# Moving the first two compressed transpositions of the next head group ahead of a turn's last gated sum and its split

## The chip, the cores and the metric

The kernel runs on one core of a Trainium2 chip. The metric is the device time of one execution in microseconds (us). Before the change the median of three runs is 2229.71 us (2229.05 to 2230.18).

## What is computed

The reference is two transformer layers (an mLSTM branch and a sliding-window attention branch, then a squared-ReLU MLP), followed by one block of sparse attention with three branches over 512 tokens and a width of 1024. Only the last block is touched here. It has 16 heads of 64 in 4 key groups of 4 heads each:

```python
q, kv, g, z = split_cols(h @ w_in, [...])
gates = jax.nn.sigmoid(g).reshape(B, S, 3, H, 1)
zs = jax.nn.silu(z).reshape(B, S, 3, H, dh)
kc = compress_kv(k_c, k_pos, k_w1, k_w2)          # 31 compressed keys
vc = compress_kv(v_c, v_pos, v_w1, v_w2)
o_cmp, p_cmp = nsa_compressed(q, kc, vc, table)   # softmax over 31 keys
sel = select_blocks(p_cmp, S)                     # S = 512 has 8 blocks, and all are taken
o_slc = nsa_selected(q, k_s, v_s, sel, table)     # so: full causal attention, keys k_s
o_win = nsa_window(q, k_w, v_w, table)            # window 512: full causal attention, keys k_w
o = jnp.stack([o_cmp, o_slc, o_win], axis=2)
y = jnp.sum(gates * o * zs, axis=2).reshape(B, S, NSA_WIDTH)
return y @ w_out
```

Everything is float32. A product is made of three passes on TensorE: both operands are split into a high part and a low rest (`hi`, `lo`), and hi x hi, lo x hi and hi x lo are summed in PSUM.

## The kernel before

**Five engines, one list of steps.** TensorE (PE), VectorE (DVE), ScalarE (ACT), GpSimd (POOL) and the queue of loads (SP) each run their own program in strict order, and semaphores join them. For the last block all of them walk one written list of steps, `NTURNS`, and each engine issues only its own share of a step. So the order of the list is the order on every engine. The list is put together by `turns()` from three tables: `NSA_FIRST` opens group 0, `NSA` is the body of groups 0 to 2 and ends with steps marked `"next"`, which belong to the group after, and `NSA_LAST` is the body of group 3. The passage from one group to the next, where steps of both alternate, is called a seam below; there are three. `('fill',)` is a slot into which `place_fill` puts the next quarter of a weight unit in a fixed sequence: `u0`, `h0`, `m1`, `u1` of `z` 0 to 5 and then of the next group's `q` 0 and 1.

**A weight unit** is a 1024 x 128 piece of the weights. A quarter of it is six 128x512 matmuls (L639 to L641). With `h0` and `u1`, ACT rounds half of the unit two further on (L1056, `w_hi`) and POOL then takes the rest (L555, `w_lo`). At `u1` of a `z` unit ACT also takes the tanh (L1103) and DVE multiplies (L1670, `sz`), which frees the PSUM bank.

**The steps by name.** `CS` the logits on the compressed keys (PE L935, 16 matmuls), then the minimum and the exponential; `cscale` sums, reciprocals and scaling of these (DVE L2144, L2145, L2150, L2151); `CT` transposes one tile of 128 tokens of them (PE L946, four matmuls), ACT copies the tile twice (L1502, L1504) and DVE subtracts for the low part (L2156); `CV` multiplies it with the values (PE L957); `cmul` adds the result into `y` (DVE L2170). `XS` is a full causal score tile (PE L967), DVE adds the bias and finds the row minimum (L2183), ACT takes the exponential (L1512); `xrec`, `xsa`, `xsp` scale it; `XT` transposes (PE L976, ACT L1525, DVE L2199), `XV` multiplies with the values (L989, L990), `xsum` adds the halves. `fmul` is the gated sum of the last branch: for the second half of the tokens DVE multiplies (L2218) and adds (L2219). `yhi` and `ylo` split `y` for the last product: for the second half ACT rounds (L1541) after L2219, and DVE takes the rest (L2222) after L1541. Nothing before the last product reads these two parts.

Score tiles use two PSUM banks in turn, and transpositions two others; a step has to wait until the consumer of the tile two before it is done. `CV` of tiles 0 and 1 waits for L2156 of its own tile. `CV` of tiles 2 and 3 waits in addition for `cmul` of tiles 0 and 1, since they share the output banks. DVE's share of `fmul` 1, `ylo` 1, `CT` and `XS` is this:

```python
elif s[0] == "CT":
    dve.wait_ge(pt_hi, pt0 + pv_index("c", qt) + 1)
    V.tensor_tensor(PTn[qt % 2][CP:CP + NC, 0, :], ps[0:NC, 4 + us[0].b, :], PTn[qt % 2][0:NC, 0, :].bitcast(F32),
                    ALU.subtract).then_inc(t_free[us[0].b], 1)
elif s == ("fmul", 1):
    link(V.tensor_tensor(ocur[:, :, cols], ocur[:, :, cols], sz[:, 4:6, cols], ALU.mult))
    V.tensor_tensor(y32[:, :, cols], y32[:, :, cols], ocur[:, :, cols], ALU.add).then_inc(y_v, 1)
elif s == ("ylo", 1):
    dve.wait_ge(y_hi_done, DEPTH * KT + it * 2 + 2)
    V.tensor_tensor(y_part(1, it, 1), y32[:, :, TOKENS[1]], y_part(0, it, 1).bitcast(F32),
                    ALU.subtract).then_inc(y_done, 1)
```

Of the kernel before, what the change touches and what calls it, by code (L numbers as in the profile page):

```python
# [72 lines left out]
def unit(kind, n):  # L73

    return [("u0", kind, n), ("h0", kind, n), ("m1", kind, n), ("u1", kind, n)]
# [51 lines left out]
        + [("TK", 2), ("TK", 3)] + unit("q", 0)[:2] + [("ngatesT",)] + unit("q", 0)[2:] + [("compress",)] + unit("q", 1))  # L127
BRANCH_PV = {"c": 0, "s": 4, "f": 14}
ITER_PV = 24
NSA_FIRST = [('ks',), ('gst',), ('kclo',), ('fill',), ('fill',), ('fill',), ('CS', 0), ('CS', 1), ('cscale', 0), ('vclo',), ('fill',), ('cscale', 1), ('fill',), ('fill',), ('gstv',)]  # L130
# [2210 lines left out]
```

## Time and profile before

| | |
|---|---|
| median of three runs | 2229.71 us |
| profiled execution | 2229.75 us, of which the span is 2228.0 us |
| PE busy | 2178.1 us (98% of the span) |
| DVE, ACT, POOL busy | 1046.1, 1085.3, 971.9 us |
| mean granted TensorE clock | 0.996 |
| CS of groups 0 to 3 starts at | 1849.52, 1928.20, 2011.44, 2094.34 us |

The profile is one execution. A row of a timeline gives the start in us from the span's start, the duration, engine, line, operation and tiles; in brackets stands the idle time of the engine just before, and the instruction that ended it. PE is busy nearly all the time, so what counts is the little idle time of PE and who ends it.

### The profile page before, as it was taken

Reading aid. Unit: us, or ns where it says so; the run is one execution under the profiler, and the core shown is the slowest. Engines: PE = TensorE matmul, PEld = TensorE weight load, DVE = VectorE, ACT = ScalarE, POOL = GpSimd, SP = SyncE. Lnnn points to the kernel's source line nnn. Section 1 sums busy time; section 2 is a strip of 40 time slices with the busy share of each in tenths; the row PEclk is TensorE's granted clock in tenths of the full one; section 3 lists DMA queues with packets and bytes.
Section 4 is the critical chain, followed back from the end, with each engine's and each line's share of the span. In section 5 each row is a group of like instructions: output and inputs, shape, how many; then the busy total and the mean of one; then the engine's idle time right before and its main releaser. Section 6 shows DMA issues by size and latency. Waiting matters only on the chain.

```text
span 2228.0 us, 31566 instructions
## 1 busy us (share of the span) xinstructions
PE 2178.1 (98%) x10287; PEld 1793.3 (80%) x10287; DVE 1046.1 (47%) x2195; ACT 1085.3 (49%) x2273; POOL 971.9 (44%) x757
## 2 busy tenths in 40 slices
PE   7999999999999999999999999999999999999997
PEld 5888888788888888888888788888888787777766
DVE  7365364523231234563563623321324726767773
ACT  5466466434232234464564624322324427787783
POOL 3333333444444444434333344544544334555544
PEclk9999999999999999999999999999999999999999
DMA  3222222223322322222322223323322431211213
GB/s 131 85 86 67 94 78 69 82 94 107 101 95 94 104 94 95 85 76 76 95 70 83 67 94 110 99 95 97 102 94 94 155 123 58 74 64 53 76 32 121
DMA packets 60288, 198.70 MB, mean 89 GB/s; under 512 B 6815, under 2 KB 13520, under 8 KB 59537
## 3 DMA queue, kind: packets, MB, share of 16 engines
q1 hardware_dynamic: 53808, 183.77, 25.2%
q10 hardware_dynamic: 6368, 13.50, 1.7%
q8 instruction: 64, 1.05, 0.2%
q14 instruction: 48, 0.39, 0.1%
HBM read 192.99 MB, written 4.26 MB: 89 GB/s over the span
## 4 chain that ended last, share of the span: by engine, by line
issue 57%; POOL 26%; PE 9%; DVE 5%; ACT 1%; POOLq 1%; DMA 0%; DVEq 0%; SPq 0%; ACTq 0%
POOL w_lo L541 26%; PE ps L639 2%; PE ps L641 2%; PE ps L640 2%; DVE Pn L2183 1%; PE ps L976 1%; PE ps L967 1%; PE ps L989 1%; DVE PTn L2199 1%; POOLq L537 1%; PE ps L990 1%; POOLq L539 1%; DMA w_raw<-w_all 0%; DVE y L2170 0%; DVE ocur L2212 0%
## 5 line engine op out<-in xcount | busy, mean ns | idle before, releaser
L541 POOL TENSOR_TENSOR w_lo<-w_raw,w_hi 128x512 fp32r<-128x512 f32 x592 | 778.4, 1322 | 1065.9 <-ACT w_hi L1056 1064.2
L639 PE MATMUL ps<-hT_hi,w_hi 128*128 128x512 f32 x1600 | 643.4, 402 | 1.9 <-DVE hT_lo L1732 1.3
L641 PE MATMUL ps<-hT_hi,w_lo 128*128 128x512 f32 x1600 | 626.0, 391 | 0.0
L640 PE MATMUL ps<-hT_lo,w_hi 128*128 128x512 f32 x1600 | 624.9, 391 | 0.0
L1056 ACT ACTIVATE w_hi<-w_raw 128x512 fp32r<-128x512 f32 x664 | 410.8, 626 | 414.1 <-PE ps L641 380.2
L641 PEld LDWEIGHTS ps<-hT_hi,w_lo 128*128 128x128 f32 x1600 | 301.0, 188 | 65.3
L639 PEld LDWEIGHTS ps<-hT_hi,w_hi 128*128 128x128 f32 x1600 | 301.5, 188 | 62.1 <-issue 2.4
L640 PEld LDWEIGHTS ps<-hT_lo,w_hi 128*128 128x128 f32 x1600 | 301.9, 189 | 57.6 <-issue 0.5
L639 PE MATMUL ps<-u_hi,w_hi 128*128 128x512 f32 x512 | 199.2, 389 | 0.0
L640 PE MATMUL ps<-u_lo,w_hi 128*128 128x512 f32 x512 | 199.2, 389 | 0.0
L641 PE MATMUL ps<-u_hi,w_lo 128*128 128x512 f32 x512 | 199.2, 389 | 0.0
L1704 DVE TENSOR_TENSOR x<-x,ps 128x512 f32<-128x512 f32 x64 | 44.0, 688 | 256.6 <-PE ps L641 256.6
L555 POOL TENSOR_TENSOR w_lo<-w_raw,w_hi 128x512 fp32r<-128x512 f32 x72 | 93.1, 1296 | 115.1 <-ACT w_hi L1056 115.1
L1677 DVE SCALAR_TENSOR_TENSOR e_buf<-ps,rs 128x512 f32<-128x512 f32 x64 | 44.3, 692 | 208.6 <-PE ps L641 208.6
L1107 ACT ACTIVATE u_hi<-e_buf 128x512 fp32r<-128x512 f32 x64 | 40.5, 633 | 173.1 <-DVE e_buf L1677 173.1
L639 PEld LDWEIGHTS ps<-u_hi,w_hi 128*128 128x128 f32 x512 | 96.1, 188 | 20.0
L640 PEld LDWEIGHTS ps<-u_lo,w_hi 128*128 128x128 f32 x512 | 96.1, 188 | 19.9
L641 PEld LDWEIGHTS ps<-u_hi,w_lo 128*128 128x128 f32 x512 | 96.1, 188 | 19.9
L1640 DVE SCALAR_TENSOR_TENSOR aq<-ps,aq 64x512 fp32r<-64x512 f32 x32 | 22.0, 689 | 149.3 <-ACT aq L1081 148.7
L1512 ACT ACTIVATE Pn<-Pn,st 128x128 f32<-128x128 f32 (+3 forms) x128 | 71.5, 559 | 25.0 <-DVE st L2183 25.0
L2183 DVE CUSTOM_DVE_ANT_0 Pn<-ps,biasn 128x128 f32<-128x128 f32 (+3 forms) x128 | 60.2, 489 | 25.2 <-DVEq L1587 24.9
L639 PE MATMUL ps<-y_hi,w_hi 128*128 128x512 f32 x176 | 68.7, 390 | 1.7 <-DVE y_lo L2222 1.7
(330 smaller groups left out, 3437.9 us busy)
## 6 DMA issues: line engine op xcount, KB each, us to landing
w_raw<-w_all SPq DMA_DIRECT2D x332, 512.0 KB, 3.3
bias<-scr_w ACTq DMA_DIRECT2D x8, 512.0 KB, 3.7
biasn<-scr_n SPq DMA_DIRECT2D x4, 1024.0 KB, 5.2
w1k<-w_in ACTq DMA_DIRECT2D x2, 1024.0 KB, 7.4
w1v<-w_in ACTq DMA_DIRECT2D x1, 2048.0 KB, 12.8
scr_x<-x ACTq DMA_DIRECT2D x1, 2048.0 KB, 7.5
x<-scr_x SPq DMA_DIRECT2D x1, 2048.0 KB, 9.2
out<-x SPq DMA_DIRECT2D x16, 128.0 KB, 1.8
```

The lines of the kernel that those rows point to most:

```text
L537: with pool.Fori(0, count) as i:
L541: nc.gpsimd.tensor_tensor(w_lo[:, h, :], raw[:, h // 2, (h % 2) * HALF:(h % 2 + 1) * HALF], w_hi[:, h, :].bitcast(F32), ALU.subtract).then ...
L555: nc.gpsimd.tensor_tensor(w_lo[:, 2 * u.b + h, :], raw[:, u.b, h * HALF:(h + 1) * HALF], w_hi[:, 2 * u.b + h, :].bitcast(F32), ALU.subtrac ...
L639: nc.tensor.matmul(ps[:, p, :], wh, hi[:, kk, :], start=(kk == 0), stop=False)
L640: nc.tensor.matmul(ps[:, p, :], wh, lo[:, kk, :], start=False, stop=False)
L641: last = nc.tensor.matmul(ps[:, p, :], wl, hi[:, kk, :], start=False, stop=(kk == KT - 1))
L1056: nc.scalar.activation(w_hi[:, 2 * p + h, :], raw[:, p, h * HALF:(h + 1) * HALF], ACT.Copy)\
L1107: nc.scalar.activation(u_hl[0][:, n, :], e_buf[:, e.b, :], ACT.Square).then_inc(u_hi_done, 1)
L1512: nc.scalar.activation(p_, p_, ACT.Exp, scale=-1.0, bias=st[:, 0, j:j + 1], accum_out=st[:, 1, j:j + 1]).then_inc(probs, 1)
L1677: V.scalar_tensor_tensor(e_buf[:, e.b, :], g, 0.0, rs[:, :], ALU.max, ALU.mult).then_inc(g_free[u.b], 1)
L1704: V.tensor_tensor(x[:, n, :], x[:, n, :], g, ALU.add).then_inc(g_free[u.b], 1)
L2183: last = V.tensor_tensor_reduce(out=Pn[:, qt % 2, hd, 0:n], in0=ps[:, 2 + b_, e * n:(e + 1) * n], in1=reverse(biasn, hd, n), scale=1.0, sc ...
```

## The change

The two `CT` steps that opened `NSA` and `NSA_LAST`, and the two fill slots beside them, are put at the end of `NSA_FIRST` and among the `"next"` steps at the end of `NSA`. In the three seams `fmul` 1 comes after them, and `yhi` 1 and `ylo` 1 after one fill slot more. In group 0 they keep their place as such, but the quarters `m1` and `u1` of `z` 1 now stand around them. The diff, cut to the places that differ (each table is one line in the source, cut by "..."):

```diff
-NSA_FIRST = [..., ('cscale', 1), ('fill',), ('fill',), ('gstv',)]
-NSA = [('fill',), ('CT', 0), ('CT', 1), ('fill',), ('XS', 's', 0, 0), ('fill',), ('XS', 's', 0, 2), ...
-       ('xsum', 'f', 3), ("next",) + ('vclo',), ('fmul', 1), ("next",) + ('fill',), ("next",) + ('cscale', 1),
-       ("next",) + ('fill',), ("next",) + ('fill',), ("next",) + ('gstv',), ('yhi', 1), ('ylo', 1)]
-NSA_LAST = [('CT', 0), ('fill',), ('CT', 1), ('fill',), ('XS', 's', 0, 0), ('XS', 's', 0, 2), ...
+NSA_FIRST = [..., ('cscale', 1), ('fill',), ('fill',), ('gstv',), ('fill',), ('CT', 0), ('CT', 1), ('fill',)]
+NSA = [('XS', 's', 0, 0), ('fill',), ('XS', 's', 0, 2), ...
+       ('xsum', 'f', 3), ("next",) + ('vclo',), ("next",) + ('fill',), ("next",) + ('cscale', 1),
+       ("next",) + ('fill',), ("next",) + ('fill',), ("next",) + ('gstv',), ("next",) + ('fill',),
+       ("next",) + ('CT', 0), ("next",) + ('CT', 1), ('fmul', 1), ("next",) + ('fill',), ('yhi', 1), ('ylo', 1)]
+NSA_LAST = [('XS', 's', 0, 0), ('XS', 's', 0, 2), ...
```

On DVE, the seam from group 0 to group 1 stands like this before, with the semaphores that each row waits for (`vector_chain` is DVE's own last result):

```order
L2128 TENSOR_TENSOR vcst<-vc,vcst 31x128 [waits cmp_staged,o_free1]
L2218 TENSOR_TENSOR ocur<-ocur,sz 128x2x256
L2219 TENSOR_TENSOR y_152<-y_152,ocur 128x2x256 [waits vector_chain]
L2144 TENSOR_REDUCE st<-Pn 128x8 [waits cmp_probs]
L2145 RECIPROCAL st<-st 128x8 [waits vector_chain]
L2150 TENSOR_TENSOR st<-st,gat 128x8 [waits vector_chain]
L2151 TENSOR_TENSOR Pn<-Pn,st 128x8x31 [waits vector_chain]
L1670 SCALAR_TENSOR_TENSOR sz<-e_buf,ps 128x512 [waits tanh_z]
L2222 TENSOR_TENSOR y_lo<-y_152,y_hi 128x2x256 [waits g_free0,y_hi_done]
L2156 TENSOR_TENSOR PTn_146<-ps,PTn_146 31x512 [waits probs_transposed_hi]
L2156 TENSOR_TENSOR PTn_147<-ps,PTn_147 31x512 [waits probs_transposed_hi]
L2183 ISA Pn,st<-ps,biasn 128x128 [waits bias_in,s_ready0,vector_chain]
```

And after, on the same engine in the same place:

```order
L2128 TENSOR_TENSOR vcst<-vc,vcst 31x128 [waits cmp_staged,o_free1]
L2144 TENSOR_REDUCE st<-Pn 128x8 [waits cmp_probs]
L2145 RECIPROCAL st<-st 128x8 [waits vector_chain]
L2150 TENSOR_TENSOR st<-st,gat 128x8 [waits vector_chain]
L2151 TENSOR_TENSOR Pn<-Pn,st 128x8x31 [waits vector_chain]
L1670 SCALAR_TENSOR_TENSOR sz<-e_buf,ps 128x512 [waits tanh_z]
L2156 TENSOR_TENSOR PTn_146<-ps,PTn_146 31x512 [waits g_free0,probs_transposed_hi]
L2156 TENSOR_TENSOR PTn_147<-ps,PTn_147 31x512 [waits probs_transposed_hi]
L2218 TENSOR_TENSOR ocur<-ocur,sz 128x2x256
L2219 TENSOR_TENSOR y_152<-y_152,ocur 128x2x256 [waits vector_chain]
L2222 TENSOR_TENSOR y_lo<-y_152,y_hi 128x2x256 [waits y_hi_done]
L2183 ISA Pn,st<-ps,biasn 128x128 [waits bias_in,s_ready0,vector_chain]
```

The gated sum and its split, three instructions that stood apart ahead of L2156, now stand together directly ahead of the first row minimum L2183. The other seams read the same.

On ACT, the same seam before (L1541 is `yhi` 1, the L1056 behind the copies belongs to quarter `h0` of `z` 1, L1512 are the exponentials of `XS`):

```order
L1487 ACTIVATE vf_hl<-vtf 128x4x64
L1541 ACTIVATE y_hi<-y_152 128x2x256 [waits y_sum]
L1502 ACTIVATE PTn_146<-ps 31x512 [waits t_ready0,probs_used]
L1504 ACTIVATE PTn_146<-PTn_146 31x512 [waits probs_transposed_hi]
L1502 ACTIVATE PTn_147<-ps 31x512 [waits t_ready1,probs_used]
L1504 ACTIVATE PTn_147<-PTn_147 31x512 [waits probs_transposed_hi]
L1056 ACTIVATE w_hi<-w_raw 128x512 [waits w_used,raw_in1]
L1512 ACTIVATE Pn,st<-Pn,st 128x128 [waits row_min_done] x4
```

And after:

```order
L1487 ACTIVATE vf_hl<-vtf 128x4x64
L1502 ACTIVATE PTn_146<-ps 31x512 [waits t_ready0,probs_used]
L1504 ACTIVATE PTn_146<-PTn_146 31x512 [waits probs_transposed_hi]
L1502 ACTIVATE PTn_147<-ps 31x512 [waits t_ready1,probs_used]
L1504 ACTIVATE PTn_147<-PTn_147 31x512 [waits probs_transposed_hi]
L1056 ACTIVATE w_hi<-w_raw 128x512 [waits w_used,raw_in1]
L1541 ACTIVATE y_hi<-y_152 128x2x256 [waits y_sum]
L1512 ACTIVATE Pn,st<-Pn,st 128x128 [waits row_min_done] x4
```

L1541 goes behind the four copies and one rounding. PE's order is the same in the first two seams. In the last one, PE's order differs by this:

```order
-L946 MATMUL ps<-ident,Pn 31x128 x4
-L639 MATMUL ps<-hT_hi,w_hi 128x512
-L640 MATMUL ps<-hT_lo,w_hi 128x512
-L641 MATMUL ps<-hT_hi,w_lo 128x512
-L639 MATMUL ps<-hT_hi,w_hi 128x512
-L640 MATMUL ps<-hT_lo,w_hi 128x512
-L641 MATMUL ps<-hT_hi,w_lo 128x512
-L946 MATMUL ps<-ident,Pn 31x128 x4
```

Before, one quarter stands between the two transpositions; after, the quarter comes first and both transpositions (`x8`) follow it. In group 0 the quarter `m1` moves ahead of the transpositions and `u1` behind them, so the tanh, the rounding and `sz` of `z` 1 move ahead of the first row minima. POOL's and SP's orders are unchanged everywhere.

## Rows read from the trace of the kernel before

**Rows 1.** The page: busy time of each engine.
```profile
PE 2178.1 (98%) x10287; PEld 1793.3 (80%) x10287; DVE 1046.1 (47%) x2195; ACT 1085.3 (49%) x2273; POOL 971.9 (44%) x757
```
**Rows 2.** PE's waits from 1500 us on: total us, times, longest.
```profile
PE ps L957 <- DVE PTn L2156: 2.6, 3, 0.9
```
**Rows 3.** Timeline of DVE, seam from group 0 to group 1.
```profile
1936.11 0.69 DVE L2218 TENSOR_TENSOR ocur<-ocur,sz 128x512 f32<-128x512 f32 x1
1936.83 1.66 DVE L2219 TENSOR_TENSOR y<-y,ocur 128x512 f32<-128x512 f32 x1
1938.41 0.40 DVE L2144 TENSOR_REDUCE st<-Pn 128x8 f32<-128x248 f32 x1
1939.08 0.17 DVE L2150 TENSOR_TENSOR st<-st,gat 128x8 f32<-128x8 f32 x1
1939.73 0.69 DVE L1670 SCALAR_TENSOR_TENSOR sz<-e_buf,ps 128x512 f32<-128x512 f32 x1
1940.57 0.69 DVE L2222 TENSOR_TENSOR y_lo<-y,y_hi 128x512 fp32r<-128x512 f32 x1 [0.15 <-DVE sz L1670]
1941.30 1.28 DVE L2156 TENSOR_TENSOR PTn<-ps,PTn 31x512 fp32r<-31x512 f32 x2
1942.61 0.29 DVE L2183 CUSTOM_DVE_ANT_0 Pn<-ps,biasn 128x128 f32<-128x128 f32 x1
```
**Rows 4.** Timeline of POOL, the same seam.
```profile
1936.47 1.48 POOL L555 TENSOR_TENSOR w_lo<-w_raw,w_hi 128x512 fp32r<-128x512 f32 x1 [0.54 <-ACT w_hi L1056]
1942.30 1.29 POOL L555 TENSOR_TENSOR w_lo<-w_raw,w_hi 128x512 fp32r<-128x512 f32 x1 [4.35 <-ACT w_hi L1056]
```
**Rows 5.** Timeline of ACT, the same seam.
```profile
1936.60 0.41 ACT L1487 ACTIVATE vf_hl<-vtf 128x256 fp32r<-128x256 f32 x1
...
1938.53 0.63 ACT L1541 ACTIVATE y_hi<-y 128x512 fp32r<-128x512 f32 x1 [1.52 <-DVE y L2219]
1939.06 0.57 ACT L1502 ACTIVATE PTn<-ps 31x512 fp32r<-31x512 f32 x1
...
1941.59 0.63 ACT L1056 ACTIVATE w_hi<-w_raw 128x512 fp32r<-128x512 f32 x1
```
**Rows 6.** Timeline of PE, the same seam.
```profile
1936.43 1.03 PE L946 MATMUL ps<-ident,Pn 128*31 128x128 f32 x8
...
1942.03 0.50 PE L957 MATMUL ps<-PTn,vcst 95*128 95x512 f32 x1 [0.95 <-DVE PTn L2156]
```
**Rows 7.** Timeline of DVE, group 2: first minima of tiles 0, 1 and 2.
```profile
2025.85 0.29 DVE L2183 CUSTOM_DVE_ANT_0 Pn<-ps,biasn 128x128 f32<-128x128 f32 x1
...
2032.08 0.42 DVE L2183 CUSTOM_DVE_ANT_0 Pn<-ps,biasn 128x256 f32<-128x256 f32 x1
...
2037.09 0.56 DVE L2183 CUSTOM_DVE_ANT_0 Pn<-ps,biasn 128x384 f32<-128x384 f32 x1 [0.30 <-DVEq L1587]
```
**Rows 8.** Timeline of PE, group 2: the last score tile of tile 2.
```profile
2038.64 0.44 PE L967 MATMUL ps<-kn_hi,qn 128*128 128x384 f32 x1 [0.25 <-DVEq L2187]
```
**Rows 9.** Timeline of DVE, seam from group 2 to group 3.
```profile
2102.52 0.69 DVE L2218 TENSOR_TENSOR ocur<-ocur,sz 128x512 f32<-128x512 f32 x1
...
2104.53 1.02 DVE L2150 TENSOR_TENSOR st<-st,gat 128x8 f32<-128x8 f32 x1
...
2108.89 0.29 DVE L2183 CUSTOM_DVE_ANT_0 Pn<-ps,biasn 128x128 f32<-128x128 f32 x1
...
2115.09 0.42 DVE L2183 CUSTOM_DVE_ANT_0 Pn<-ps,biasn 128x256 f32<-128x256 f32 x1 [0.45 <-DVEq L1587]
```
**Rows 10.** Timeline of POOL, the same seam.
```profile
2104.24 1.29 POOL L555 TENSOR_TENSOR w_lo<-w_raw,w_hi 128x512 fp32r<-128x512 f32 x1 [1.90 <-ACT w_hi L1056]
```
**Rows 11.** Timeline of PE, the same seam.
```profile
2102.84 0.60 PE L946 MATMUL ps<-ident,Pn 128*31 128x128 f32 x4
...
2104.67 0.60 PE L946 MATMUL ps<-ident,Pn 128*31 128x128 f32 x4
```
**Rows 12.** Stretches of 2 us: PE, PEld, DVE, ACT, POOL busy, clock, DMA, GB/s.
```profile
2096.00:2098.00 2.00, 2.00 (x8) 1.63 (x8) 1.86 (x6) 0.93 (x2) 1.26 (x2) 0.59 0.36 135
```

More of the change, by code:

```diff
@@ L129 @@
 ITER_PV = 24
-NSA_FIRST = [('ks',), ('gst',), ('kclo',), ('fill',), ('fill',), ('fill',), ('CS', 0), ('CS', 1), ('cscale', 0), ('vclo',), ('fill',), ('cscale', 1), ('fill',), ('fill',), ('gstv',)]
-NSA = [('fill',), ('CT', 0), ('CT', 1), ('fill',), ('XS', 's', 0, 0), ('fill',), ('XS', 's', 0, 2), ('CV', 0), ('fill',), ('CV', 1), ('cmul', 0), ('CT', 2), ('xrec', 's', 0), ('xsp', 's', 0), ('fill',), ('CT', 3), ('xsa', 's', 0), ('fill',), ('XS', 's', 1, 0), ('XS', 's', 1, 2), ('fill',), ('CV', 2), ('cmul', 1), ('xrec', 's', 1), ('XT', 's', 0, 0), ('vlo',), ('fill',), ('CV', 3), ('xsa', 's', 1), ('XS', 's', 2, 0), ('fill',), ('xsp', 's', 1), ('XS', 's', 2, 1), ('XS', 's', 2, 2), ('XS', 's', 2, 3), ('cmul', 2), ('cmul', 3), ('fill',), ('xrec', 's', 2), ('XT', 's', 1, 0), ('XV', 's', 0, 0), ('XT', 's', 1, 1), ('xsa', 's', 2), ('XS', 's', 3, 0), ('XS', 's', 3, 1), ('fill',), ('XV', 's', 1, 0), ('XS', 's', 3, 2), ('xsp', 's', 2), ('XS', 's', 3, 3), ('xsum', 's', 0), ('XV', 's', 1, 1), ('kf',), ('XT', 's', 2, 0), ('xrec', 's', 3), ('xsp', 's', 3), ('fill',), ('xsum', 's', 1), ('XT', 's', 2, 1), ('fill',), ('fill',), ('XV', 's', 2, 0), ('XT', 's', 2, 2), ('fill',), ('xsa', 's', 3), ('XS', 'f', 0, 0), ('XS', 'f', 0, 2), ('XV', 's', 2, 1), ('xrec', 'f', 0), ('XV', 's', 2, 2), ('xsp', 'f', 0), ('XT', 's', 3, 0), ('XT', 's', 3, 1), ('fill',), ('fill',), ('xsum', 's', 2), ('XV', 's', 3, 0), ('XT', 's', 3, 2), ('xsa', 'f', 0), ('XV', 's', 3, 1), ('smul', 0), ('XT', 's', 3, 3), ('XS', 'f', 1, 0), ('fill',), ('XS', 'f', 1, 2), ('XV', 's', 3, 2), ('xrec', 'f', 1), ('xsp', 'f', 1), ('fill',), ('XT', 'f', 0, 0), ('fill',), ('xsa', 'f', 1), ('XS', 'f', 2, 0), ('XS', 'f', 2, 1), ('fill',), ('XS', 'f', 2, 2), ('XV', 's', 3, 3), ('XS', 'f', 2, 3), ('xrec', 'f', 2), ('XT', 'f', 1, 0), ('xsum', 's', 3), ('XV', 'f', 0, 0), ('XT', 'f', 1, 1), ('fill',), ('xsa', 'f', 2), ('xsp', 'f', 2), ('XS', 'f', 3, 0), ('XS', 'f', 3, 1), ('fill',), ('XV', 'f', 1, 0), ('XS', 'f', 3, 2), ('XS', 'f', 3, 3), ('XV', 'f', 1, 1), ('xrec', 'f', 3), ('xsum', 'f', 0), ('xsp', 'f', 3), ('XT', 'f', 2, 0), ('XT', 'f', 2, 1), ('fill',), ('smul', 1), ('xsa', 'f', 3), ('fill',), ('XV', 'f', 2, 0), ('XT', 'f', 2, 2), ('xsum', 'f', 1), ("next",) + ('ks',), ('XV', 'f', 2, 1), ('fill',), ('XT', 'f', 3, 0), ('fill',), ('XV', 'f', 2, 2), ('XT', 'f', 3, 1), ('xsum', 'f', 2), ('fill',), ('XV', 'f', 3, 0), ("next",) + ('gst',), ("next",) + ('kclo',), ('XV', 'f', 3, 1), ('XT', 'f', 3, 2), ('fmul', 0), ("next",) + ('fill',), ('XT', 'f', 3, 3), ('yhi', 0), ("next",) + ('CS', 0), ("next",) + ('CS', 1), ('ylo', 0), ("next",) + ('cscale', 0), ('XV', 'f', 3, 2), ('XV', 'f', 3, 3), ('xsum', 'f', 3), ("next",) + ('vclo',), ('fmul', 1), ("next",) + ('fill',), ("next",) + ('cscale', 1), ("next",) + ('fill',), ("next",) + ('fill',), ("next",) + ('gstv',), ('yhi', 1), ('ylo', 1)]
```

4 lines of the change are left out of this document (3 added, 1 removed).

## The prediction

> **What bounds the kernel now.** The page comes first: PE is busy for 98% of the span [rows 1], so only PE's idle time can be won, and only work that makes PE wait can lose. Next come PE's waits in the last block. One group of them belongs to the place of the change: L957, the first product with the compressed values, waits three times, 2.6 us in all, for DVE's L2156 [rows 2]. One of these is the 0.95 us in the seam from group 0 to group 1 [rows 6]. The rest are one in the next seam and one in group 0; the last seam has none. The timelines of the seam tell why. DVE works without a break from 1936.11 to 1943: gated sum, `cscale`, `sz`, split, and only then L2156 [rows 3]. Its input was there long before, since the transposition began at 1936.43 [rows 6].
>
> The same rows show a cost that is not work. L2219 took 1.66 us, L2218, the same shape, 0.69 [rows 3]. POOL's L555 ran from 1936.47 to 1937.95 [rows 4], and L2219, begun at 1936.83, ended at 1938.49, 0.54 after it. L2150, 8 elements wide, took 0.17 us while POOL was idle [rows 3, 4] and 1.02 us in the last seam, where it ended at 2105.55 and POOL's L555 at 2105.53 [rows 9, 10]. So a DVE instruction with both inputs in SBUF that starts during an L555 waits for its end and then does nearly its whole work. L1670, with an input in PSUM, has no such case in these rows.
>
> **What drives PE behind the seam.** Call M the start of the first L2183 of a group. In group 2 M is 2025.85, the first minimum of tile 1 starts at M + 6.23, that of tile 2 at M + 11.24 [rows 7], and PE's last score tile of tile 2 starts at 2038.64, M + 12.79, released by DVE [rows 8]. In between DVE waits only for exponentials and a tanh that themselves follow M. I take this chain to be rigid: when M moves, the tile moves with it, however early PE is. In group 2 PE gets there just in time, so it has nothing in reserve that a late M could use.
>
> **Seams 1 and 2, walked.** DVE: with the gated sum gone, L2144 starts at 1936.11 in place of 1938.41. From L2144 to L2150 it is 0.67 us [rows 3], so L2150 wants to start at 1936.78, inside POOL's L555, which began at 1936.47 [rows 4] and, with no L2218 in its way, lasts 1.29. It is held to 1937.78. L2151, L1670 and its own completion take as long as before: from the end of L2150 at 1939.25 to L2222 at 1940.57 it was 1.32 [rows 3], so L2156 starts at 1939.10. The pair takes 1.31 (1941.30 to 1942.61), to 1940.41. ACT is ready for it: L1487 is done at 1937.01 and the first four transpositions at 1936.43 + 0.60 = 1937.03 [rows 6, 11], so L1502 starts at about 1937.10 and the rounding L1056 2.53 later (1939.06 to 1941.59 [rows 5]), at 1939.63. It ends at 1940.26, and POOL follows 0.08 later, as 1942.22 was followed by 1942.30 [rows 4, 5]: 1940.34 to 1941.63.
>
> So the gated sum, free to start at 1940.41, meets an L555 again. If POOL is first, L2218 ends 0.54 behind 1941.63, at 1942.17, and L2219 at 1942.88. If L2218 is first, the pair takes what it took before, 2.38 (1936.11 to 1938.49), to 1942.79. Then comes a round trip that nothing covers: L1541 on ACT (0.04 + 0.63), then L2222, 0.73 to the next start. M is 1942.88 + 0.67 + 0.03 + 0.73 = 1944.3, against 1942.61 [rows 3]: +1.7 us. DVE paid one collision before; now it pays two (0.9 and 1.2) and waits 0.7 for ACT, and of these 2.8 us the 0.97 that L2219 lost before and small rests go off.
>
> PE gains first. L957 needs the first L2156, done at 1939.8, and starts without its 0.95 us wait. Then it loses: with M 1.7 us late, the tile at M + 12.79 is 1.7 us late, and the 0.95 is idle time a few us on. Net +1.7 us a seam, +3.4 for two. Cheapest case: no second collision, M late by 0.6 or so. Dearest: +2.4, a full L555 more.
>
> The Trainium skill speaks of this port. "SBUF — State Buffer", section on its two sides, says that a VectorE instruction with two SBUF inputs and a GpSimd instruction exclude each other for the whole instruction, and whichever starts first keeps the port pair. By that rule the trace's 1.66 and 1.02 us are expected [rows 3, 9], and a tie at 1940.4 would go either way for 0.1 us. The rule speaks against a change that lays DVE's pair behind a rounding by ACT.
>
> **The last seam.** L2144 can start at 2102.52, where L2218 stood [rows 9], and `cscale` is over before POOL's L555 at 2104.24 [rows 10]. But both transpositions now stand behind a quarter. Four transpositions and the quarter took 1.83 before (2102.84 to 2104.67 [rows 11]); by the eight of 1.03 [rows 6] less the 0.60 of four, four hold PE for 0.43 or less, so the first begins about 1.4 later, at 2104.2, and ends 0.60 on. L1502 starts at about 2104.88, the rounding 2.53 later at 2107.41, and POOL's next L555 at 2108.12, to 2109.41. The second L2156 follows the second L1502 and ends at 2107.4; L2218 runs 2107.43 to 2108.12 and L2219 is held until 2109.41 + 0.54 = 2109.95. With the round trip M is 2109.95 + 1.43 = 2111.4 against 2108.89: +2.5. Before, DVE waited 0.45 for PE ahead of the minima of tile 1 [rows 9], and that gap takes up 0.45: net +2.0. Should L2219 slip in ahead of POOL, 1.1 less, +0.9.
>
> **Group 0.** No gated sum stands there. L957 could save the 0.7 that is left of the 2.6 [rows 2, 6]: 2.6 less two waits of 0.95. But tanh, rounding and `sz` of `z` 1 now come ahead of the minima, M is 1.4 later, and the chain behind M is shorter by about that and a little more. Between 0 and -0.7; I take -0.3.
>
> **Sum.** 1.7 + 1.7 + 2.0 - 0.3 = +5.1 us. 2229.75 + 5.1 = 2234.85 for the profiled execution; it stands 0.04 over the median of 2229.71, so 2234.8.
>
> **Hidden edits.** L1541 moved by itself costs nothing, as ACT is idle there (1.52 us before it [rows 5]); it costs through L2222 alone. The `y` parts are read at the very end, so their delay is free, and the three instructions as such are as many as before. The loads have the earlier rounding to follow and are not late.
>
> **Rivals.**
> - *The cover holds* (not slower). If the pair of L2156 is what mattered, and the tiles behind have the slack that I deny, PE keeps 0.95 + 0.95 + 0.7 = 2.6 us: 2227.1. For it: L957 is the only wait of the seams that the change aims at, and it does go. Against: the chain of rows 7 and 8 ends in a PE wait as it is, so no slack stands there. It decides if M is not over 0.6 late, about what PE has gained less its own wait. Chance 0.13.
> - *One collision fewer.* The gated sum or `cscale` passes an L555 by a few tenths, in both first seams, and in the last L2219 comes first: +0.7 to +0.9 a seam, -0.3, +2.2 in all: 2231.9. For it: the starts of DVE and POOL are 0.07 us apart in my walk. Against: the pair is 1.4 us long, an L555 1.29, and either order costs about the same. Chance 0.17.
> - *The clock.* In the last seam the granted clock was 0.59 over two us, that is 1.2 GHz for part of it, behind PE's thin work on the compressed logits [rows 12]. PE now idles 2 us more behind each seam. Two us at 0.59 cost 0.8 us, and with a like stretch behind it I estimate 1.8 for one such fall. One or two more such stretches: 2236.6 to 2238.4. If the one of before goes, the last seam gives back about 0.9. Chance of one more 0.10.
> - The forecast as it stands has 0.60.
>
> **How the numbers follow.** Two tenths of a per cent, 4.5 us, is what a measurement can tell here, so the line to "slower" is 2234.2, and the forecast stands 0.6 above it. Of its 0.60 about 0.43 lies above the line and 0.17 below; the clock's 0.10 lies above; the rivals at 2227.1 and 2231.9 are within 0.2%. A gain of 4.5 us would need the whole 2.6 and the clock's 1.8 together: 0.02. So faster 0.02, same 0.45, slower 0.53. The range reaches down to 2230.0, leaving out most of the first rival, and up to 2237.4 (+2.4 twice, +2.5, a part of a slow stretch).
>
> **What would show it.** In the profile after, the 0.95 us before L957 are gone in the first two seams. L2150 takes about 1.0 us there, and L2218 and L2219 together about 2.4 or more. ACT's L1541 is followed by L2222 with an idle DVE of 0.7 before it. The first L2183 of groups 1 and 2 comes 1.7 us later from its CS than before (14.4 us there), and PE waits over 1 us in all between L957 of tile 2 and the third score tile of tile 2. It is wrong if M moves as said and PE has no new waits, or if L2150 and the gated sum run at 0.17 and 1.4 us.

## The result, and the profile after

The changed kernel takes 2235.5 us in the median against 2230.07 us for the kernel before, measured beside it: a ratio of 1.0024, 95% interval 1.0017 to 1.0031. It is slower by 0.24%. The forecast was 2234.8 us in a range from 2230.0 to 2237.4, with "slower" as the likeliest of the three outcomes. The profiled span grew from 2228.0 to 2233.5 us, by 5.5; the forecast's sum was +5.1.

First the page's busy times, the line that answers to [rows 1]. No engine has more instructions. PE's 2 us more go with one more stretch at half clock, in which its matmuls are longer.

```profile
PE 2180.2 (98%) x10287; PEld 1794.4 (80%) x10287; DVE 1044.8 (47%) x2195; ACT 1085.1 (49%) x2273; POOL 970.4 (43%) x757
```

DVE in the seam from group 0 to group 1, to be held against [rows 3]; the columns are start, duration, engine, line, tiles and, in brackets, the idle time before and who ended it:

```profile
1937.55 0.97 DVE L2150 TENSOR_TENSOR st<-st,gat 128x8 f32<-128x8 f32 x1
...
1939.85 1.28 DVE L2156 TENSOR_TENSOR PTn<-ps,PTn 31x512 fp32r<-31x512 f32 x2 [0.15 <-ACT PTn L1502]
1941.16 1.81 DVE L2218 TENSOR_TENSOR ocur<-ocur,sz 128x512 f32<-128x512 f32 x1
1943.01 0.69 DVE L2219 TENSOR_TENSOR y<-y,ocur 128x512 f32<-128x512 f32 x1
1944.40 0.69 DVE L2222 TENSOR_TENSOR y_lo<-y,y_hi 128x512 fp32r<-128x512 f32 x1 [0.70 <-ACT y_hi L1541]
1945.01 0.28 DVE L2183 CUSTOM_DVE_ANT_0 Pn<-ps,biasn 128x128 f32<-128x128 f32 x1
```

POOL in the same seam, against [rows 4]:

```profile
1937.22 1.28 POOL L555 TENSOR_TENSOR w_lo<-w_raw,w_hi 128x512 fp32r<-128x512 f32 x1 [0.53 <-ACT w_hi L1056]
1941.14 1.29 POOL L555 TENSOR_TENSOR w_lo<-w_raw,w_hi 128x512 fp32r<-128x512 f32 x1 [2.63 <-ACT w_hi L1056]
```

Everything on DVE is as walked. L2150, 8 elements wide, ends with the first L555 after 0.97 us. L2218 starts 0.02 us behind the second L555 and ends 0.54 us after it; before, that was L2219's share [rows 3, 4]. Then DVE stands for 0.70 us until ACT has rounded `y`. Group 1 begins CS at 1928.96, so its first row minimum comes 16.05 us later; it was 14.41.

PE in the same seam, against [rows 6 and 8]. The column is the same; "issue" means that no releaser was found.

```profile
1941.68 0.47 PE L957 MATMUL ps<-PTn,vcst 95*128 95x512 f32 x1
...
1950.49 0.50 PE L957 MATMUL ps<-PTn,vcst 95*128 95x512 f32 x1 [0.73 <-DVE PTn L2156]
1951.67 0.63 PE L976 MATMUL ps<-ident,Pn 128*128 128x128 f32 x4 [0.68 <-POOL Pn L582]
...
1954.66 0.47 PE L957 MATMUL ps<-PTn,vcst 95*128 95x512 f32 x1 [0.97 <-issue]
...
1958.13 0.45 PE L967 MATMUL ps<-kn_hi,qn 128*128 128x384 f32 x1 [0.25 <-DVEq L2187]
```

The wait of 0.95 us is gone, and PE reaches the scores of tile 1 1.14 us earlier, at 18.29 us after CS. It waits three times further on, 2.38 us in all, and each time DVE's work is behind it. The first is L2156 of tile 2. The second is called POOL, but POOL's L582 had itself waited for DVE's L2194. The one called "issue" is DVE as well: the product L2170 of tile 1 ran from 1953.70 for 0.86 us, and L957 starts 0.10 us behind its end. The last score tile of tile 2 comes 29.17 us after CS. It was 27.54.

The waits of PE and DVE from 1500 us on (total, times, longest) show the trade, to be read beside [rows 2]:

```profile
PE ps L957 <- DVE PTn L2156: 3.0, 3, 1.9
PE ps L957 <- issue: 2.3, 3, 1.0
DVE y_lo L2222 <- ACT y_hi L1541: 2.8, 4, 0.7
```

The wait that the change removes is again at the head of the list, but now it is another L957, that of tile 2.

The last seam, DVE and PE, against [rows 9]:

```profile
2110.58 1.83 DVE L2218 TENSOR_TENSOR ocur<-ocur,sz 128x512 f32<-128x512 f32 x1
...
2114.44 0.28 DVE L2183 CUSTOM_DVE_ANT_0 Pn<-ps,biasn 128x128 f32<-128x128 f32 x1
...
2120.22 0.42 DVE L2183 CUSTOM_DVE_ANT_0 Pn<-ps,biasn 128x256 f32<-128x256 f32 x1
```

```profile
2119.64 0.50 PE L957 MATMUL ps<-PTn,vcst 95*128 95x512 f32 x1 [1.88 <-DVE PTn L2156]
...
2128.39 0.44 PE L967 MATMUL ps<-kn_hi,qn 128*128 128x384 f32 x1 [0.25 <-DVEq L2187]
```

**The time by stretches.** From CS of a group to the last score tile of its tile 2, and from there to the next CS, each read in both traces:

| stretch | before | after | difference | forecast |
|---|---|---|---|---|
| start to CS of group 0 | 1849.52 | 1849.76 | +0.24 | 0 |
| group 0 | 23.35 | 23.86 | +0.51 | -0.3 |
| seam 0 to 1 | 27.54 | 29.17 | +1.63 | +1.7 |
| seam 1 to 2 | 27.20 | 28.83 | +1.63 | +1.7 |
| seam 2 to 3 (a stretch at half clock in each) | 28.18 | 30.01 | +1.83 | +2.0 |
| rest of groups 0, 1, 2 | 55.33, 55.70, 55.70 | 55.34, 55.70, 55.72 | +0.03 | 0 |
| behind the last one, to the end | 105.48 | 105.11 | -0.37 | 0 |

What a seam loses is neither won back nor added to in the 55.7 us behind it. That is what makes offsets from CS a usable ruler below: where no stretch at half clock lies in them, they repeat to a few hundredths, while the medians have an interval of about 0.1%, 2 us.

**The last seam without a slow stretch.** The granted clock was 0.50 to 0.68 from 2096 to 2100 us before the change [rows 12] and 0.50 to 0.74 from 2120 to 2124 after it, so this row of the table mixes the order with the clock. Two kernels of experiment 8 have the seams of the kernel before, and both profiles have a clock of 1.00 all through the last one. In the first of them its CS starts at 2095.88:

```profile
2104.52 1.66 DVE L2221 TENSOR_TENSOR y<-y,ocur 128x512 f32<-128x512 f32 x1
2110.29 0.29 DVE L2185 CUSTOM_DVE_ANT_0 Pn<-ps,biasn 128x128 f32<-128x128 f32 x1
```

```profile
2109.72 0.50 PE L959 MATMUL ps<-PTn,vcst 95*128 95x512 f32 x1 [0.86 <-DVE PTn L2158]
...
2123.59 0.44 PE L969 MATMUL ps<-kn_hi,qn 128*128 128x384 f32 x1 [0.25 <-DVEq L2189]
```

The old last seam is then like the other two: L2219 (here L2221) meets an L555, the first minimum comes at 14.41, L957 (here L959) has its wait, and the score tile comes at 27.71. The second profile has 14.41 and 27.71 too. So 0.47 of the 28.18 belong to the slow stretch. After the change the first minimum stands at 16.06, and from there to the score tile it is 13.21 us where the clock stays up (experiment 2), 13.95 in this profile. That makes 29.27 for the new order: it costs 1.56 here, much as in the other seams. The +1.83 is 1.56 of order and 0.74 less 0.47 of clock.

### The profile page after: what moved, and what is told of

Same layout as the page of the kernel before. It is cut to its first block, busy times and chain, and to the rows that moved or that the text cites. A ratio compares the mean times of both kernels' runs of the same rounds, so it can differ in the third digit from the quotient of the medians.

```text
span 2233.5 us, 31566 instructions
## 1 busy us (share of the span) xinstructions
PE 2180.2 (98%) x10287; PEld 1794.4 (80%) x10287; DVE 1044.8 (47%) x2195; ACT 1085.1 (49%) x2273; POOL 970.4 (43%) x757
## 4 chain that ended last, share of the span: by engine, by line
issue 57%; POOL 26%; PE 8%; DVE 6%; ACT 2%; POOLq 1%; ACTq 0%; DVEq 0%
POOL w_lo L541 25%; DVE Pn L2183 1%; PE ps L639 1%; PE ps L641 1%; PE ps L640 1%; PE ps L976 1%; DVE PTn L2199 1%; PE ps L967 1%; PE ps L989 1%; POOLq L537 1%; POOLq L539 1%; PE ps L990 1%; ACT Pn L1512 0%; DVE sz L1670 0%; DVE y L2170 0%
## 5 line engine op out<-in xcount | busy, mean ns | idle before, releaser
L1056 ACT ACTIVATE w_hi<-w_raw 128x512 fp32r<-128x512 f32 x664 | 410.9, 626 | 414.7 <-PE ps L641 384.2
L555 POOL TENSOR_TENSOR w_lo<-w_raw,w_hi 128x512 fp32r<-128x512 f32 x72 | 92.7, 1290 | 119.8 <-ACT w_hi L1056 119.8
L1512 ACT ACTIVATE Pn<-Pn,st 128x128 f32<-128x128 f32 (+3 forms) x128 | 71.4, 559 | 26.2 <-DVE st L2183 26.2
L2183 DVE CUSTOM_DVE_ANT_0 Pn<-ps,biasn 128x128 f32<-128x128 f32 (+3 forms) x128 | 60.2, 489 | 25.3 <-DVEq L1587 25.1
```

The source lines that it names most:

```text
L555: nc.gpsimd.tensor_tensor(w_lo[:, 2 * u.b + h, :], raw[:, u.b, h * HALF:(h + 1) * HALF], w_hi[:, 2 * u.b + h, :].bitcast(F32), ALU.subtrac ...
L1056: nc.scalar.activation(w_hi[:, 2 * p + h, :], raw[:, p, h * HALF:(h + 1) * HALF], ACT.Copy)\
L1512: nc.scalar.activation(p_, p_, ACT.Exp, scale=-1.0, bias=st[:, 0, j:j + 1], accum_out=st[:, 1, j:j + 1]).then_inc(probs, 1)
L2183: last = V.tensor_tensor_reduce(out=Pn[:, qt % 2, hd, 0:n], in0=ps[:, 2 + b_, e * n:(e + 1) * n], in1=reverse(biasn, hd, n), scale=1.0, sc ...
```

## Experiments

My theory, A throughout: DVE's instructions ahead of the first row minimum set it, and PE follows 13.1 us behind. The main rivals: PE's earlier transpositions are a gain that something else hides; the clock makes the difference. Kernels add lines above the functions, so that a line number in their rows is higher by 2 to 18; the tiles tell which instruction it is. `order` is the list of steps of the last block. In the quoted expectations e4_sum_behind_minima is the kernel of experiment 5 and e5_group0_alone the first of experiment 8.

### 1. Group 0 put back

```
+    i = order.index((0, ("gstv",)))
+    order[i + 1:i + 8] = [(0, ("CT", 0)), (0, ("CT", 1)), (0, ("XS", "s", 0, 0)), (0, F), (0, ("XS", "s", 0, 2)), (0, ("CV", 0)), (0, F)]
```

> The changed kernel with the start of group 0 put back into its old order; the three passages between groups stay changed. Theory A (rigid chain: what the first row minimum loses is lost at the end): the changed profile showed group 0 0.52 us longer from its first CS matmul to its last compressed scores, so this kernel is 0.5 us faster than the changed one, +4.9 us on the kernel before (ratio 1.0022), and POOL's L575 no longer lies beside the small L2194 of group 0. Theory B (my prediction's own term): the new start of group 0 gained 0.3 us, so this kernel is 0.3 us slower than the changed one, +5.7 us (1.0026). Theory C (most of the loss is the shifted clock fall, not the order): under +3 us.

Ratio 1.0019 [1.0010, 1.0028] beside the changed kernel's 1.0024 [1.0017, 1.0031]: the intervals overlap, so the times alone cannot tell the two apart. The offsets can. Group 0's last score tile of tile 2, from CS at 1849.95:

```profile
1873.27 0.44 PE L969 MATMUL ps<-kn_hi,qn 128*128 128x384 f32 x1 [0.24 <-DVEq L2189]
```

That is 23.32 us, as before the change, and the stretch from CS 0 to CS 1 is 78.63 us, against 79.20 changed and 78.68 before. So group 0's new order costs 0.5 us, and the three seams carry the other nine tenths: A holds, C falls. In the changed kernel two rows name the collision in group 0, on DVE and on POOL:

```profile
1869.88 0.56 DVE L2194 TENSOR_TENSOR st<-st,gat 128x4 f32<-128x4 f32 x1
```

```profile
1869.69 0.73 POOL L575 TENSOR_TENSOR vf_hl<-vtf,vf_hl 128x256 fp32r<-128x256 f32 x1
```

L2194, 4 elements wide, takes 0.16 us with the old order.

### 2. The next rounding behind the split: no second collision

As experiment 1, and

```
+    for g in range(NG - 1):
+        i = order.index((g, ("fmul", 1)))
+        order[i + 1:i + 4] = [(g, ("yhi", 1)), (g, ("ylo", 1)), (g + 1, F)]
```

> As the first kernel (group 0 old), and at each passage the fill step that follows the gated sum stands behind yhi 1 and ylo 1. ACT then rounds y (L1541) before the next fill quarter's L1056, and POOL's L555 of that quarter comes after L2218 instead of beside it. TensorE's order is unchanged. Theory A (collision on the path): L2218 falls from 1.82 to 0.69 us, the first row minimum comes 1.1 us earlier than in the changed kernel (CS+14.9 at the first two passages, was 16.05, before 14.41), each passage costs 0.5 us instead of 1.65 to 1.83: +1.5 us on before, ratio 1.0007. Theory B (the second collision is covered, the ACT round trip alone sets the minimum): minimum unchanged at CS+16.0, ratio 1.0022 as the first kernel.

Ratio 1.0005 [0.9996, 1.0014]. The gated sum, the wait and the first minimum of group 1, CS at 1928.46:

```profile
1940.66 0.69 DVE L2223 TENSOR_TENSOR ocur<-ocur,sz 128x512 f32<-128x512 f32 x1
...
1942.78 0.69 DVE L2227 TENSOR_TENSOR y_lo<-y,y_hi 128x512 fp32r<-128x512 f32 x1 [0.70 <-ACT y_hi L1546]
1943.39 0.28 DVE L2188 CUSTOM_DVE_ANT_0 Pn<-ps,biasn 128x128 f32<-128x128 f32 x1
```

The minimum stands at 14.93, the score tile of tile 2 at 28.05, 0.51 later than before. Taking a POOL instruction away from beside L2218 gave back 1.12 us of 1.63. PE's order is the same as in experiment 1. The collision was on the path; B falls.

### 3. The split's rest behind the row minima: no wait for ACT

As experiment 1, and `ylo` 1 (L2222) of each group behind the next group's `XS s 0 2`; `move(step, after)` takes a step out and puts it behind another.

```
+    for g in range(NG - 1):
+        move((g, ("ylo", 1)), (g + 1, ("XS", "s", 0, 2)))
```

> As the first kernel (group 0 old), and ylo 1 (DVE L2222) stands behind the next group's step XS s 0 2, where DVE had 1.2 us idle, so DVE waits for ACT's rounding no more ahead of the first minimum; the collision of L2218 with L555 stays. Theory A: the minimum comes 0.70 (wait) + 0.69 (L2222) = 1.4 us earlier than in the changed kernel: CS+14.65, 0.25 later than before; each passage costs about 0.25 us: +0.8 us on before, ratio 1.0003. Theory B (DVE is not what the row minimum waits for; ACT or TensorE is late next): the minimum moves by under 0.7 us and the time stays at 1.0015 or above.

Ratio 1.0001 [0.9992, 1.0010]. The first minimum came at 14.66, as A had it. But the score tile of tile 2 stands at 28.05 in the first seam, 0.51 behind the kernel before, not 0.25:

```profile
1943.91 0.28 DVE L2192 CUSTOM_DVE_ANT_0 Pn<-ps,biasn 128x128 f32<-128x128 f32 x1
...
1945.38 0.69 DVE L2231 TENSOR_TENSOR y_lo<-y,y_hi 128x512 fp32r<-128x512 f32 x1
1946.71 0.69 DVE L1679 SCALAR_TENSOR_TENSOR sz<-e_buf,ps 128x512 f32<-128x512 f32 x1 [0.64 <-ACT e_buf L1112]
```

L2222 itself is free there, in DVE's idle time. But ACT now rounds `y` (0.63 us) behind the start of the minima, so its exponentials and the tanh that `sz` waits for come later: `sz` is 2.80 us behind the first minimum, where it was 2.54. So the first minimum is not the whole path. ACT's queue behind it is, too.

### 4. Transpositions early, gated sum where it was

As experiment 1, with `fmul` 1 put back behind `vclo`, and `yhi` 1 and `ylo` 1 behind `CT` 1:

```
+    for g in range(NG - 1):
+        for s in ("fmul", 1), ("yhi", 1), ("ylo", 1):
+            order.remove((g, s))
+        i = order.index((g + 1, ("vclo",)))
+        order.insert(i + 1, (g, ("fmul", 1)))
+        i = order.index((g + 1, ("CT", 1)))
+        order[i + 1:i + 1] = [(g, ("yhi", 1)), (g, ("ylo", 1))]
```

> The changed kernel with group 0 old, and in every passage fmul 1 where it stood before (ahead of cscale 1) and yhi 1 and ylo 1 right behind CT 1, ahead of the fill step: the transpositions move as in the change, the gated sum does not. Theory A (VectorE's work ahead of the first minimum sets the chain, and TensorE's earlier transpositions are worth nothing by themselves): VectorE has the same instructions ahead of the minimum as before with no idle time between them, so the minimum stays at CS+14.4 +-0.2, the times at ratio 1.0000, and TensorE gives back its 0.95 us at its next wait for VectorE. Theory B (the transpositions are a gain that the moved sum hid): 0.9 us gained at each of the first two passages, ratio 0.9992 or less. Theory C (the transpositions ahead themselves cost): 1.0010 or more.

Ratio 0.9999 [0.9990, 1.0008]. Group 1 has its CS at 1927.69; on DVE

```profile
1936.33 1.66 DVE L2228 TENSOR_TENSOR y<-y,ocur 128x512 f32<-128x512 f32 x1
...
1942.19 0.28 DVE L2192 CUSTOM_DVE_ANT_0 Pn<-ps,biasn 128x128 f32<-128x128 f32 x1
```

and on PE

```profile
1940.80 0.50 PE L966 MATMUL ps<-PTn,vcst 95*128 95x512 f32 x1 [0.19 <-DVE PTn L2165]
1951.84 0.47 PE L966 MATMUL ps<-PTn,vcst 95*128 95x512 f32 x1 [0.86 <-issue]
1955.30 0.44 PE L976 MATMUL ps<-kn_hi,qn 128*128 128x384 f32 x1 [0.24 <-DVEq L2196]
```

The targeted wait of 0.95 shrinks to 0.19, PE is 0.72 earlier at the scores of tile 1 (18.71 after CS), waits 0.86 at the L957 behind them, and is at 27.61 for tile 2, where it was 27.54. The moved transpositions are worth nothing by themselves, and cost nothing. The loss belongs to the gated sum and its split: moving the fill quarter (`h0`) from ahead of the split to behind it gives 1.12 us of the 1.63 (experiment 2), and moving the sum back as well gives 1.56.

### 5. The gated sum moved the other way

The kernel before, with `fmul` 1 behind the next group's `CV` 0 and `yhi` 1, `ylo` 1 behind the fill step after it:

```
+    for g in range(NG - 1):
+        for s in ("fmul", 1), ("yhi", 1), ("ylo", 1):
+            order.remove((g, s))
+        i = order.index((g + 1, ("CV", 0)))
+        j = order.index((g + 1, F), i)
+        order[i + 1:j + 1] = [(g, ("fmul", 1))] + order[i + 1:j + 1] + [(g, ("yhi", 1)), (g, ("ylo", 1))]
```

> The kernel before with its compressed transpositions where they were, and the last gated sum (fmul 1) moved the other way: behind the next group's CV 0, with yhi 1 and ylo 1 behind the fill step after it. TensorE's order is that of before. Theory A (the first minimum sets the chain): L2218, L2219, L2222 leave the stretch ahead of the minimum; the minimum comes 2.2 us earlier than before, but TensorE's own matmuls then bound: about 0.95 us gained at each of the first two passages and up to 1 at the last: -2 to -3 us, ratio 0.9990. Theory B (the sum only moves the delay to the product of tile 0, L2170, which TensorE's next matmul waits for): time within 0.5 us of before, ratio 1.0000.

Ratio 0.9999 [0.9990, 1.0009]: a miss for A's number. The first minimum did come 2.2 us earlier (12.20 after CS), yet the tile 2 scores only 0.12. DVE, behind the minima:

```profile
1940.36 0.69 DVE L2225 TENSOR_TENSOR y<-y,ocur 128x512 f32<-128x512 f32 x1
1941.14 0.69 DVE L1676 SCALAR_TENSOR_TENSOR sz<-e_buf,ps 128x512 f32<-128x512 f32 x1
1942.18 1.35 DVE L2228 TENSOR_TENSOR y_lo<-y,y_hi 128x512 fp32r<-128x512 f32 x1 [0.35 <-ACT y_hi L1547]
1944.06 0.86 DVE L2176 TENSOR_TENSOR y<-ps,sz 64x256 f32<-64x256 f32 x2 [0.53 <-DVE y_lo L2228]
```

The sum met the same two costs in the new place: 0.35 us for ACT, and 0.66 beside an L555 that began at 1941.70. The minima of tile 1, behind them, came 0.12 us earlier (20.88), not 2.2. B has the time of this run right, though not the tile: PE waits 0.97 us at L957 of tile 3, which starts 0.10 behind the end of DVE's product L2170 of tile 1, not of tile 0.

### 6. The same, the split ahead of the fill step

```
-        j = order.index((g + 1, F), i)
-        order[i + 1:j + 1] = [(g, ("fmul", 1))] + order[i + 1:j + 1] + [(g, ("yhi", 1)), (g, ("ylo", 1))]
+        order[i + 1:i + 1] = [(g, ("fmul", 1)), (g, ("yhi", 1)), (g, ("ylo", 1))]
```

> As the kernel with the sum behind the minima (e4_sum_behind_minima), with yhi 1 and ylo 1 now ahead of the fill step instead of behind it. There L2222 waited 0.35 us for ACT's rounding and lasted 1.35 us beside POOL's L555. Theory A (these two are on the chain to the minima of tile 1): L2222 lasts 0.69 us and the minima of tile 1 come 0.3 to 0.9 us earlier than there (20.88 after CS at the first passage), the compressed scores of tile 2 as much earlier: 0.3 to 0.9 us per passage, ratio to before 0.9990 to 0.9997. Theory B (ACT's later tanh L1103 and roundings take the place): minima of tile 1 within 0.2 us, ratio 0.9999.

Here `yhi` 1 and `ylo` 1 stand directly behind `fmul` 1. Ratio 0.9996 [0.9987, 1.0005]. CS of group 1 is at 1926.86:

```profile
1942.71 0.69 DVE L2227 TENSOR_TENSOR y_lo<-y,y_hi 128x512 fp32r<-128x512 f32 x1 [0.70 <-ACT y_hi L1546]
```

The collision is gone, the wait is 0.70. Minima of tile 1 at 20.50, scores of tile 2 at 27.03, 0.39 earlier than in experiment 5, and 0.51 earlier than before the change. A's lower end.

### 7. The same, with `sz` in the gap

The step order of experiment 5, and on ACT alone the rounding of the weight quarter (L1056) behind that of `y`, the tanh L1103 still ahead. `LATE` holds the three places.

```
+                    if place[0] in LATE:
+                        store(s, cur[s[1:]])
+                        place.append(cur[s[1:]])
...
+                        if len(place) > 1:
+                            u = place.pop()
+                            split(u.n + 2, u.m + 1, u.b, 1)
```

> As the kernel with the sum behind the minima (e4_sum_behind_minima), but on ACT alone the rounding of the next weight quarter (L1056) of the fill step there stands behind y's rounding (L1541), while the tanh L1103 stays ahead of it. Theory A (VectorE's chain from the first minimum to the minima of tile 1 sets the passage): VectorE forms sz (L1670) while ACT rounds y, L2222 then waits for nothing and POOL's L555 comes after it; against the kernel with the split before the fill (tile 1's minima 20.50 after CS, compressed scores of tile 2 at 27.03 at the first passage) both come 0.5 us earlier: 1.0 us per passage earlier than before, -3 us in all, ratio 0.9986. Theory B (TensorE's own matmuls bound by now, since its last wait there was 0.36 to 0.70 us): tile 1's minima come earlier, tile 2's scores by at most 0.4 to 0.7 us more than before's 0.5: ratio 0.9990 to 0.9993.

2225.95 us; ratio 0.9977 [0.9968, 0.9986] to the kernel before. It beats both kernels. CS of group 1 is at 1927.12:

```profile
1942.36 0.69 DVE L1688 SCALAR_TENSOR_TENSOR sz<-e_buf,ps 128x512 f32<-128x512 f32 x1
1943.19 0.69 DVE L2240 TENSOR_TENSOR y_lo<-y,y_hi 128x512 fp32r<-128x512 f32 x1
1944.41 0.86 DVE L2188 TENSOR_TENSOR y<-ps,sz 64x256 f32<-64x256 f32 x2 [0.53 <-DVE y_lo L2240]
...
1947.13 0.42 DVE L2201 CUSTOM_DVE_ANT_0 Pn<-ps,biasn 128x256 f32<-128x256 f32 x1
```

```profile
1950.20 0.47 PE L966 MATMUL ps<-PTn,vcst 95*128 95x512 f32 x1 [0.22 <-issue]
1953.67 0.45 PE L976 MATMUL ps<-kn_hi,qn 128*128 128x384 f32 x1 [0.25 <-DVEq L2205]
```

`sz` fills the gap in which ACT rounds `y`, L2222 waits for nothing, and POOL's L555 starts at 1943.54, behind L2222's start. Minima of tile 1 at 20.01, scores of tile 2 at 26.55: each 0.5 earlier than in experiment 6, as A said. By the offsets the three seams give 0.99, 1.00 and, against the 27.71 of the last seam without a slow stretch, 0.97 us: 3.0 in all, as forecast. That is 0.13%, just outside the interval of the measured 0.23% (0.14 to 0.32%). What makes up the rest is not known.

### 8. Group 0 alone, twice

The kernel before with group 0 in the new order:

```
+    i = order.index((0, ("gstv",)))
+    order[i + 1:i + 8] = [(0, F), (0, ("CT", 0)), (0, ("CT", 1)), (0, F), (0, ("XS", "s", 0, 0)), (0, ("XS", "s", 0, 2)), (0, ("CV", 0))]
```

> The kernel before with only the start of group 0 in the changed order; the three passages are those of before. Theory A (what the changed profile showed in group 0): the first row minimum 1.7 us later (CS+12.2, was 10.54), the minima of tile 1 within 0.1 us, L2194 of tile 0 0.56 us long beside POOL's L575, and the compressed scores of tile 2 0.5 us later: +0.5 us, ratio 1.0002. Theory B (my prediction's term): -0.3 us, ratio 0.9999. The times can't tell these apart; the profile's offsets from the first CS matmul can.

> The same kernel as e5_group0_alone once more, for a profile in which the fall of TensorE's clock does not lie in group 0. Theory A (group 0's new order costs by itself, with the gated sum nowhere near): from its first CS matmul the first row minimum comes at +12.2, L2194 of tile 0 takes 0.56 us beside POOL's L575, and the third score tile of tile 2 comes at +23.9 us, 0.5 later than before's +23.35. Theory B (my prediction's term, or no effect): +23.0 to +23.4.

The first gave 1.0006 [0.9997, 1.0014]; the second is a single look (2232.71 us, beside one run of the kernel before at 2226.17), too little for a ratio. In both a stretch at a granted clock of 0.50, 1.2 GHz, lies in group 0 behind CS (between 1850 and 1855), so neither offset can be held against 23.86: the score tile came at 25.49 and 25.45. Two other kernels with the old group 0 had such a stretch there too, and stood at 24.37 and 24.36 (experiments 2 and 7). Held against those, the new order costs 1.1 us, and L2194 again takes 0.57. So group 0's order costs by itself, 0.5 us undisturbed (experiment 1) and 1.1 beside a slow stretch.

### The seams side by side

Offsets from CS of group 1 in us; no slow stretch lies in any of these rows.

| kernel | first minimum | minima of tile 1 | scores of tile 2 | ratio |
|---|---|---|---|---|
| before | 14.41 | 21.00 | 27.54 | 1 |
| changed | 16.05 | 22.63 | 29.17 | 1.0024 |
| 1, group 0 old | 16.05 | 22.63 | 29.17 | 1.0019 |
| 2, no second collision | 14.93 | 21.52 | 28.05 | 1.0005 |
| 3, no wait for ACT | 14.66 | 21.52 | 28.05 | 1.0001 |
| 4, sum early | 14.50 | 21.08 | 27.61 | 0.9999 |
| 5, sum behind the minima | 12.20 | 20.88 | 27.42 | 0.9999 |
| 6, split ahead of the fill | 12.20 | 20.50 | 27.03 | 0.9996 |
| 7, `sz` in the gap | 12.20 | 20.01 | 26.55 | 0.9977 |

From the minima of tile 1 to the scores of tile 2 it is 6.53 to 6.54 us in all nine. That part is the rigid one.

## Why the prediction was right, and where it was not

- **Seams 1 and 2: right.** +1.63 each against +1.7. Both collisions, 0.97 and 1.81 us, and the 0.70 us for ACT are there. Experiment 2 took away one and got 1.12 of the 1.63 back; experiment 4 took away the sum's move and got back nearly all of it (0.07 left).
- **The chain that PE cannot outrun: right for this change, too broad as stated.** From the first minimum to the scores of tile 2 it is 13.1 us wherever nothing of the sum stands in between (before, changed, 1, 2, 4), for PE early or late. Experiments 3 and 5 moved the minimum and not the scores as much. What is fixed begins at the minima of tile 1; ahead of them the distance is what DVE and ACT have queued. The rival "the cover holds" is refuted by experiment 4: PE's gain of 0.7 there brings no time.
- **The last seam: sum nearly right, its parts not.** I had the first minimum 2.5 us later; it is 1.5 (16.06 against 14.55 after CS), as L2218 met the whole L555 and no L2219 was caught. DVE no longer waited for PE ahead of tile 1's minima, and 1.09 remained there (21.84 against 20.75), so this 0.45 went as I said. But I had walked this seam from a profile in which a stretch at 1.2 GHz lay in it, and took its rows for what the order does. In the two undisturbed seams of experiment 8 L2219 does meet an L555, L957 does wait, and DVE does not wait the 0.45. Against them the order costs 1.56, not 2.0. That +1.83 was measured is partly luck: a slow stretch worth 0.74 fell into this seam after the change, and one worth 0.47 before it.
- **Group 0: wrong.** -0.3 forecast, +0.51 measured. I took the chain behind a later minimum to be "shorter by about that and a little more". It is shorter by 1.66: minima of tile 1 at 16.82, before 16.79. The little more is not there. And I had not looked two steps on, where the shifted steps lay L2194 beside POOL's L575 (0.40 us). With 0.04 at tile 1 and 0.07 ahead of L2194 that is the 0.51.
- **The clock: about 0.3 us of the seams, and noise at the ends.** The stretches at half clock lie in other places in each profile (one to three between 1600 and 2170 us, in kernels of either speed). My price of 1.8 us for one was too high. Where the same steps ran with and without one, it cost from 0.15 us (the seam from group 0 to group 1 in the second profile of experiment 8, 27.69 against 27.54) to 1.6 (group 0 in the new order, 25.49 against 23.86), mostly 1.0 or less. The +0.24 ahead of group 0 is within what the same code does elsewhere: CS of group 0 starts between 1847.2 and 1850.5 us in the eleven profiles. Behind the last score tile the five profiles with a slow stretch between 2156 and 2165 us need 106.1 to 106.2 us. Of the six without, five need 105.0 to 105.2, the changed kernel's among them, and only the kernel before needs 105.48. So the -0.37 looks like an accident of its one profile; no run isolates it. The effect of the stretches on the medians was not isolated.

The error of group 0 (+0.8) and the ends (-0.1) against the sizes of the seams (-0.3) make 5.1 into 5.5.

## What to carry to other kernels

A wait of the busiest engine is worth only what the chain behind it lets through: PE's 0.95 us came back as waits 9 us later, since DVE and ACT set the next stop. When an instruction moves, walk what will lie beside it on the engine that it collides with, here POOL, and what has to be rounded elsewhere before its result can be used; here these two made the loss of the seams. The same two costs, kept off DVE's chain in the opposite move by letting independent work (`sz`) stand in the gap, gave a kernel 0.23% faster than before, of which the offsets account for 0.13%. And before a seam is walked from one profile, look at its clock: one slow stretch had changed which instructions met in the last seam.

## What the runs showed of the hardware

A DVE instruction with two inputs in SBUF that meets an L555 of POOL ends 0.54 us after it, at 512 elements a row (L2218 in three seams, 1.81 to 1.83 us; 0.69 without). At 8 or 4 elements it ends with it or a little behind, and takes 0.97 or 0.56 us where it takes 0.17 or 0.16. The Trainium skill, "SBUF — State Buffer", in its section on the two separate sides, says that whichever starts first gets the shared port pair for the whole instruction and the other fully blocks. Who waits agrees with it: in experiment 7 POOL's instruction came second, 0.35 us behind L2222, and took 1.50 us instead of 1.29:

```profile
1943.54 1.50 POOL L564 TENSOR_TENSOR w_lo<-w_raw,w_hi 128x512 fp32r<-128x512 f32 x1 [2.95 <-ACT w_hi L1065]
```

"For the whole instruction" holds less exactly. L2222 ended at 1943.88, and 1.29 us from there would be 1945.17, where POOL ended at 1945.04; L2218's 0.54 after POOL's end is short of its own 0.69. The second of the two comes out 0.13 to 0.15 us short of a full wait and its full work; what it does in that time no run here shows.

A stretch at 1.2 GHz (granted clock 0.50 for about 3.5 us) cost 1.0 us in group 0 in the old order (24.37 against 23.35 us) and 0.5 in the last seam in the old order (28.18 against 27.71).
